# One core, fox and dilated attention step: the root table loaded first, the norm a tile ahead of V, first down weights in two halves, y stored from SP, and the dilated groups combined over two token halves

## The reference, cut to what matters

```python
xn = rmsnorm(xp, g_mix); fq, fk, fv, flf, dq, dk, dv, gf, gd = mixer_inputs(xn, pos, w_in, b_fgate)
o_fox = fox_prompt(fq, fk, fv, flf)                  # 8 heads, causal, with forget gates
for g, (win, dil) in enumerate(DIL_PATTERNS):        # (128,1), (512,4), (2048,16), 4 heads each
    o, lse = dil_group_prompt(dq[g], dk[g], dv[g], win, dil)
w = softmax(stack(lses), axis=0); o_dil = sum(w[..., None] * stack(outs), axis=0)
xp = xp + (sigmoid(gf) * (o_fox @ w_br_fox) + sigmoid(gd) * (o_dil @ w_br_dil)) @ w_mix_out
xp = xp + cross_attn(rmsnorm(xp, g_xattn), mkv, w_xq, w_xo)
u = rmsnorm(xp, g_ffn) @ w_up; gate, val = split(conv3(u) + b_conv)    # 2 x 2816 columns
xp = xp + (gelu(gate) * val) @ w_down
y = rmsnorm(xp, g_final)
```

## Time and profile before

| | |
|---|---|
| time, median of 3 runs | 2958.41 us (2953.82 to 2959.67) |
| profiled execution: its time, its span | 2956.13 us, 2954.2 us |
| mean granted TensorE clock | 0.988 |
| busy share of the span: PE, DVE, ACT, POOL | 98%, 29%, 19%, 5% |
| PE's part of the chain that ended last | 94% |
| mean DMA rate | 94 GB/s |

### The profile page before, as it was taken

One profiled execution on the slowest core, in us unless ns is written; L12 is line 12 of the kernel. 1 busy time (PEld: TensorE's weight loads), 2 busy tenths in 40 slices (PEclk: granted clock), 3 DMA queues, 4 the chain that ended last, 5 costly groups with the idle time before them and its releaser, 6 DMA issues.

```text
span 2954.2 us, 36649 instructions
## 1 busy us (share of the span) xinstructions
PE 2887.2 (98%) x14164; PEld 1836.5 (62%) x14164; DVE 843.3 (29%) x2149; ACT 562.8 (19%) x1247; POOL 146.8 (5%) x275
## 2 busy tenths in 40 slices
PE   7999999999989999999999999999999999999998
...
DMA packets 196065, 276.98 MB, mean 94 GB/s; under 512 B 20317, under 2 KB 136174, under 8 KB 194854
## 3 DMA queue, kind: packets, MB, share of 16 engines
...
...
## 4 chain that ended last, share of the span: by engine, by line
PE 94%; DMA 3%; DVE 2%; issue 1%; SPq 0%; ACT 0%; ACTq 0%; POOL 0%; DVEq 0%; POOLq 0%
PE psum L2289 22%; PE psum L2435 11%; PE psum L923 10%; PE psum L1817 8%; PE psum L1901 7%; PE psum L508 4%; PE psum L2053 4%; PE psum L678 3%; PE psum L1241 3%; PE psum L694 3%; PE psum L1825 3%; PE psum L1277 2%; PE psum L1257 2%; PE psum L705 2%; PE psum L2027 2%; DMA arena<-in_cache_fox_kv 1%
## 5 line engine op out<-in xcount | busy, mean ns | idle before, releaser
L2289 PE MATMUL psum<-arena 128*128 128x288 f32 (+1 forms) x2112 | 646.8, 470 | 0.0
L2289 PEld LDWEIGHTS psum<-arena 128*128 128x128 f32 x2112 | 402.4, 191 | 244.0 <-issue 170.2
L2435 PE MATMUL psum<-arena 128*128 128x256 f32 (+1 forms) x1760 | 327.2, 360 | 1.5 <-DMA arena<-in_w_down 1.5
L923 PE MATMUL psum<-arena 128*128 128x512 f32 (+3 forms) x960 | 316.9, 481 | 1.4 <-ACT arena L561 1.4
L2435 PEld LDWEIGHTS psum<-arena 128*128 128x128 f32 (+1 forms) x1760 | 287.9, 180 | 40.5 <-issue 3.8
L1817 PE MATMUL psum<-arena 128*128 128x368 f32 (+1 forms) x768 | 304.2, 496 | 1.7 <-ACT arena L1853 1.1
L1901 PE MATMUL psum<-arena 128*128 128x512 f32 x512 | 237.0, 596 | 0.8 <-issue 0.8
L923 PEld LDWEIGHTS psum<-arena 128*128 128x128 f32 (+1 forms) x960 | 195.0, 250 | 62.4 <-issue 35.1
L1817 PEld LDWEIGHTS psum<-arena 128*128 128x128 f32 x768 | 125.1, 193 | 68.7 <-issue 46.8
L754 DVE CUSTOM_DVE_ANT_0 arena<-psum,arena 128x256 f32<-128x256 f32 (+2 forms) x224 | 95.1, 456 | 213.7 <-PE psum L678 213.6
L728 ACT ACTIVATE arena<-arena 128x256 f32<-128x256 f32 (+4 forms) x192 | 107.5, 562 | 234.8 <-DVE arena L754 232.3
...
## 6 DMA issues: line engine op xcount, KB each, us to landing
arena<-in_cache_fox_kv SPq DMA_DIRECT2D x128, 256.0 KB, 4.4
arena<-in_cache_fox_kv ACTq DMA_DIRECT2D x128, 256.0 KB, 4.4
...
```

Source lines behind the costliest of these rows:

```text
L923: last = pe.matmul(banks[c0 // 512][p0:p0 + r, 0:n], xn_tile(k, g, t), wD[g][:, k, w0:w0 + n], start=(k == 0), stop=(k == KD - 1))
L2289: last = pe.matmul(banks[(u % 2) * 4 + x][:, 0:cw], wu[u % 3][:, k, :], xnT[:, k, c0:c0 + cw], start=(k == 0), stop=(k == KD - 1))
L2435: last = pe.matmul(banks[u % 2][p0:p0 + r, 0:n], hT(f)[:, t * P:t * P + r], wd[q % 2][:, f, c0:c0 + n], start=(f == 0), stop=(f == NF - 1))
```

## The change

Seven edits. (1) ACT does one Sqrt on a constant after its loads are issued, before the first Square. (2) norm1 becomes (-4, 68), which makes PE's order N0, N1, V0, N2, V1, N3, V2 and so on; wV comes in two halves with a semaphore each. (3) The transposes and copies of the past forget gates move from the pair j = 2 to j = 3. (4) The combination works on two halves of 512 tokens, on partitions 0 to 3 and 32 to 35: 36-column transposes for two of the groups (8 each, 16 for the third), PSUM banks of their own for the first two groups, all of the chain on 36 x 512, the head rows doubled at partition 32, and cleared statistics. (5) The last MLP unit goes over k outside the chunks and tells after k = 2 and k = 5; wd[0] is loaded in two halves at these two points, into the parts of xnT that are done with. (6) `down_pe` starts at once, waits for each half and, at the last f of the first tile, for the last gating; the four convout steps follow the tiles 1, 3, 5 and 7. (7) SP stores y in place of POOL.

```diff
         sel[hh, hh // 2, 64 * (hh % 2):64 * (hh % 2) + 64] = 1
+        sel[32 + hh] = sel[hh]
     c["head_rows"] = sel.reshape(P, -1)
...
 PLAN = dict(
-    norm1=(0, 63), v=(10, 82), p0=(82, 112), sums=(92, 93),
+    norm1=(-4, 68), v=(10, 82), p0=(82, 112), sums=(92, 93),
     p1=(112, 174), a0=(114, 176), p2=(174, 236), a1=(178, 238), p3=(236, 298), a2=(240, 300),
...
         s_clear = sem("block_diagonals_cleared")
+        stats_all = take(96 * NG, f0 + 6144 + 192)
         vrows = take(4 * P, f0).rearrange("p (a c) -> p a c", a=4)
...
                           .rearrange("p o h -> p (o h)")).then_inc(s_bfg, 16)
+            act.wait_ge(s_clear, 4)
+            act.activation(std[:, TT * 5 - 1:TT * 5], eps_t, ACT.Sqrt)
 
...
             pool.memset(eps_t, EPS).then_inc(s_clear, 1)
+            pool.memset(stats_all, 0.0).then_inc(s_clear, 1)
             pool.memset(qbF, 0.0).then_inc(s_clear, 1)
...
                 if t == 2:
-                    sp.dma_start(wV, w_in[:, :, O_FV:O_FV + 520]).then_inc(fp["wv_in"], 16)
+                    for h in range(2):
+                        sp.dma_start(wV[:, 4 * h:4 * h + 4, :],
+                                     w_in[:, 4 * h:4 * h + 4, O_FV:O_FV + 520]).then_inc(fp[f"wv_in{h}"], 16)
                 if t >= 5:
...
                 pe.wait_ge(*nth(n1, "kept", 2 * (t + 1)))
-                if t == 0:
-                    pe.wait_ge(fp["wv_in"], 16)
                 if t == 1:
...
                 for k in range(KD):
+                    if t == 0 and k % 4 == 0:
+                        pe.wait_ge(fp[f"wv_in{k // 4}"], 16)
                     xk = xnT[:, k, t * P:t * P + r]
...
                 last.then_inc(fp["computed"], 1)
-                if kind == "k" and j == 2 and n < 2:
+                if kind == "k" and j == 3 and n < 2:
                     yield now(start + 0.95 / 6.6)
...
                         pe.wait_ge(s_lf, 16 * NB * NPG)
-                        pe.wait_ge(fp["k_kept"], 6)
+                        pe.wait_ge(fp["k_kept"], 9)
                     else:
...
                         pe.wait_ge(fp["k_kept"], g)
-                    if g == 6:
+                    if g == 9:
                         pe.wait_ge(fp["lf_kept"], 2)
...
                 conv_rows_dve(dve)
-            for n in range(2 if j == 2 else 0):
+            for n in range(2 if j == 3 else 0):
                 yield now((n + 1.1) / 6.6)
...
         accT = take(NG * 2 * S, f0 + 22016).rearrange("p (g j t) -> p g j t", g=NG, j=2)
-        NM_d = [take(32, st0 + 192 + 64 * g) for g in range(NG)]
-        L_d = [take(32, st0 + 224 + 64 * g) for g in range(NG)]
+        NM_d, L_d = [[take(48, st0 + 192 + 48 * (2 * g + a)) for g in range(NG)] for a in range(2)]
+
+        def stat_place(g):
+
+            def place(i):
+                u = i // HD
+                half, x = ((u // 4, u % 4), (u % 2, u // 2), (0, u))[g]
+                return 32 * half + HD * x + i % HD
+            return place
+
 
...
             att_dil.append(attention([dil_unit(g, x) for x in range(2 * NQ)], [p[:, 0:256] for p in Pb], PT,
-                                     NM_d[g], L_d[g], GM_f, False, out_pairs, due))
-
-        stT = take(NG * 2 * S, f0).rearrange("p (g a t) -> p g a t", g=NG, a=2)
-        low = take(S, f0 + 7680)
-        den = take(S, f0 + 8704)
+                                     NM_d[g], L_d[g], GM_f, False, out_pairs, due, stat_place(g)))
+
+        HALF, RH = S // 2, 32 + HD
+        stT = take(NG * 2 * HALF, f0).rearrange("p (g a t) -> p g a t", g=NG, a=2)
+        low = take(HALF, f0 + 7680)
+        den = take(HALF, f0 + 8704)
         prod = [take(512, f0 + 9728 + 512 * i) for i in range(3)]
         cb = sems("combine", "turned natural shifted expd weighted own scaled spread product first second")
-        STAT = [psum[:, 3 * 512:5 * 512], psum[:, 5 * 512:7 * 512]]
+        STAT = [[banks[3], banks[4]], [banks[5], banks[6]], [psum[:, 3 * 512:5 * 512], psum[:, 5 * 512:7 * 512]]]
 
...
                     pe.wait_ge(fb["rows_dve"], 1)
-                if g:
-                    pe.wait_ge(cb["natural"], 2 * g)
+                    pe.wait_ge(s_clear, 4)
+                if g == 2:
+                    pe.wait_ge(cb["natural"], 4)
                 for a, st in enumerate((NM_d[g], L_d[g])):
-                    for u in range(NQ):
-                        last = pe.transpose(STAT[a][0:HD, u * P:(u + 1) * P], st[:, u * HD:(u + 1) * HD], ident)
+                    rows, n = ((RH, NQ // 2), (RH, NQ // 2), (HD, NQ))[g]
+                    for x in range(n):
+                        last = pe.transpose(STAT[g][a][0:rows, x * P:(x + 1) * P], st[:, x * HD:x * HD + rows], ident)
                 last.then_inc(cb["turned"], 1)
...
                         pe.wait_ge(cb["product"], m - 3)
-                    pe.matmul(banks[3 + m % 4], cst["head_rows"][0:HD, j * P:(j + 1) * P],
-                              stT[0:HD, g, 0, c * 512:(c + 1) * 512], start=True, stop=True).then_inc(cb["spread"], 1)
+                    pe.matmul(banks[3 + m % 4], cst["head_rows"][32 * c:32 * c + HD, j * P:(j + 1) * P],
+                              stT[32 * c:32 * c + HD, g, 0, :], start=True, stop=True).then_inc(cb["spread"], 1)
 
...
             act.wait_ge(cb["shifted"], NG)
-            act.activation(stT[0:HD, :, 0, :], stT[0:HD, :, 0, :], ACT.Exp).then_inc(cb["expd"], 1)
+            act.activation(stT[0:RH, :, 0, :], stT[0:RH, :, 0, :], ACT.Exp).then_inc(cb["expd"], 1)
 
...
                     att_over(dve, att_dil[NG - 1])
+                    dve.memset(stT[0:RH, 2, 0, :], 0.0)
+                    dve.memset(stT[0:RH, 2, 1, :], 1.0)
                 dve.wait_ge(cb["turned"], g + 1)
                 for a in range(2):
-                    dst = stT[0:HD, g, a, :]
-                    src = STAT[a][0:HD, :]
-                    if g:
-                        dst = dst.rearrange("p (i s) -> p s i", s=(1, 4, 8)[g])
-                        src = src.rearrange("p (s i) -> p s i", s=(1, 4, 8)[g])
-                    dve.tensor_copy(dst, src).then_inc(cb["natural"], 1)
-            nm = [stT[0:HD, g, 0, :] for g in range(NG)]
-            ls = [stT[0:HD, g, 1, :] for g in range(NG)]
-            lo, dn = low[0:HD, :], den[0:HD, :]
+                    if g == 0:
+                        last = dve.tensor_copy(stT[0:RH, 0, a, :], STAT[0][a][0:RH, :])
+                    elif g == 1:
+                        last = dve.tensor_copy(stT[0:RH, 1, a, :].rearrange("p (i s) -> p s i", s=4),
+                                               STAT[1][a][0:RH, :].rearrange("p (s i) -> p s i", s=4))
+                    else:
+                        halves = STAT[2][a].rearrange("p (s h i) -> p h s i", s=8, h=2)
+                        for h in range(2):
+                            last = dve.tensor_copy(stT[32 * h:32 * h + HD, 2, a, :].rearrange("p (i s) -> p s i", s=8),
+                                                   halves[0:HD, h])
+                    last.then_inc(cb["natural"], 1)
+            nm = [stT[0:RH, g, 0, :] for g in range(NG)]
+            ls = [stT[0:RH, g, 1, :] for g in range(NG)]
+            lo, dn = low[0:RH, :], den[0:RH, :]
             yield now(0.42)
...
                     pe.wait_ge(mp["uncopied"], u - 1)
-                for x, (c0, cw) in enumerate(CHUNKS):
+                if u < NU2 - 1:
+                    for x, (c0, cw) in enumerate(CHUNKS):
+                        for k in range(KD):
+                            last = pe.matmul(banks[(u % 2) * 4 + x][:, 0:cw], wu[u % 3][:, k, :], xnT[:, k, c0:c0 + cw],
+                                             start=(k == 0), stop=(k == KD - 1))
+                else:
                     for k in range(KD):
-                        last = pe.matmul(banks[(u % 2) * 4 + x][:, 0:cw], wu[u % 3][:, k, :], xnT[:, k, c0:c0 + cw],
-                                         start=(k == 0), stop=(k == KD - 1))
+                        for x, (c0, cw) in enumerate(CHUNKS):
+                            last = pe.matmul(banks[(u % 2) * 4 + x][:, 0:cw], wu[u % 3][:, k, :], xnT[:, k, c0:c0 + cw],
+                                             start=(k == 0), stop=(k == KD - 1))
+                        if k in (2, 5):
+                            last.then_inc(mp["chunk_read"], 1)
                 last.then_inc(mp["computed"], 1)
...
         def down_sp(sp):
-            sp.wait_ge(mp["computed"], NU2)
-            sp.dma_start(wd[0], w_dn[:, :, 0:256]).then_inc(dn["s"]["w_in0"], 16)
+            for h in range(2):
+                sp.wait_ge(mp["chunk_read"], h + 1)
+                sp.dma_start(wd[0][:, 11 * h:11 * h + 11, :], w_dn[:, 11 * h:11 * h + 11, 0:256]).then_inc(s_first[h], 16)
             sp.wait_ge(mp["tap2"], 2 * NU2)
...
                 sp.dma_start(wd[q % 2], w_dn[:, :, 256 * q:256 * q + 256]).then_inc(dn["s"][f"w_in{q % 2}"], 16)
+            for t in range(TT):
+                sp.wait_ge(s_out, t + 1)
```

(26 more changed lines are left out.)

20 lines of the change are left out of this document (11 added, 9 removed).

## The result

The changed kernel takes 2934.06 us (median of 5 runs, 2931.55 to 2940.43) against 2953.82 (5 runs, 2950.84 to 2959.67): ratio 0.9934, 95% interval 0.9914 to 0.9954, so a gain of 19.5 us, with 13.6 to 25.4 by the interval. These five runs of the kernel before are on the low side: in the later batches its median is 2958.2 to 2959.75. The prediction was 2933, range 2922 to 2943. The sum of its terms was 23.5 us; the two profiled executions differ by 24.6 (2956.13 and 2931.55).

The account below looks back on a forecast made before the run. PE was taken as the bound, with 94% of the chain that ended last; 4.0 + 1.8 + 5.5 + 2.4 + 9.5 + 0.3 = 23.5 us off the profiled 2956.13 gave 2932.6, predicted as 2933, range 2922 to 2943.

Parts of the forecast that it names:

- The start: Up to V2's first product: 4.0 us gained, bounds 2.0 to 4.6, with DVE's first reciprocal at 9.5.
- Past forget gates: Transposes moved a pair later: cost 0, bounds -1 to +1; left in place they would give back 4 us.
- The combination's transposes and idle time: Before the first spread: 1.8 us from 16 fewer transposes and 5.5 from the closed idle, margin 1.1.
- Rival C: Combination stays on the path, its chain on 36 x 512 no shorter than on 4 x 1024: 2940 us, chance 0.04.
- The combination's clock: After the spreads' batches: 2.4 us gained, bounds -2.0 to 9.7, with a fall of 2.4 lost after the first batch.
- Rival A: The clock holds through the combination, giving 9.7 us in place of 2.4: 2925 us, chance 0.14.
- Down: From the last MLP unit to the first down tiles: 9.5 us gained, 9.8 less 0.3 for g_final; bounds 7.0 to 9.8.
- g_final: Load that DVE's add waits for before down tile u = 2: landing near 2624, cost 0.3 us, bounds 0 and 1.5.
- the half microsecond: Sign at the down step: no wait of over half a microsecond before tile u = 2.
- The store: Last store of y, issued by a hardware queue in place of POOL: 0.3 us gained, bounds -1 to +1.
- a change of the mean clock outside the combination of over 0.002: Sign named in advance, for the whole program outside the combination: such a change would make the prediction wrong.
- Rival D: Slower: the clock falls elsewhere as edits shift 4-row and 8-row products in time; a doubled loss gives 2968 us, chance 0.03.

Follow-up runs that it names:

- s4_lf2: The changed kernel with the past forget gates turned in pair 2 again instead of pair 3: 2935.74 us (6 runs), ratio to before 0.9916.
- t2_before_rows4: The kernel before with the combination's 4-row spreads run over 128 rows, its idle of 5.48 us unchanged: 2959.18 us, one execution.
- t3_rows8: The changed kernel with only the 8-row bias products of the pair stages run over 128 rows: 2913.87 us in one execution; timed later, 2919.89 us (6 runs).
- r1_rows: The changed kernel with both the 8-row bias products and the 4-row spreads run over 128 rows, the others zero: 2918.24 us (6 runs), ratio to before 0.9864.
- r3_gfinal_first: The changed kernel with g_final's load issued ahead of the second quarter of the down weights: 2932.31 us, one execution.
- s3_down: The kernel before with only the down edits (last MLP unit over k, first weights in halves, early down tiles): 2951.25 us (12 runs), ratio 0.9972.

## Why the prediction was right, point by point

**What bounds the kernel.** PE's 94% of the chain stayed 94%, and what was edited off PE's path showed up in the time at the very end only, in the store.

**The start: 4.0, measured 3.15.** The mechanism was right, the bias row that holds the reciprocal included. Mis-sized: its landing. I took the 6.4 us of the earlier trace rows from the old issue; it was issued 0.1 later, took 7.0, and the reciprocal was at 10.13 and not 9.5. That is 0.6 of the 0.85. It should have been priced as one of many transfers in flight: over the thirteen executions in which it stayed last in ACT's queue it took 6.4 to 7.3 us. Whether the second transfer of wV slows it isn't shown; the four without edit 2 had 6.4 to 6.8.

**Past forget gates: 0, measured 0**, but with a wrong account of what happens without the edit (s4_lf2), and without the wait of up to 3.9 us that the kernel before has here in other executions.

**The combination's transposes and idle time: 7.3, measured 7.3.** The chain was priced step by step, and its end was right: with the 12.2 us won by then, the reciprocal forecast for 830.7 would be at 818.5, it is at 818.58; the first spread, forecast for 837.3, would be at 825.1, it is at 825.12. The margin was 1.3 us, forecast 1.1. Exp took 1.48 us, priced at no more than 2.76, and it didn't matter: DVE waited 3.23 us for the gate's products, ahead of the operation before the reciprocal, which is the wait that the forecast had named. Rival C (the chain no shorter) is refuted: 0.68 for an operation on 36 x 512, 3.34 for the reciprocal.

**The combination's clock: 2.4, measured 0.** This is the step that failed. It had one mean fall after the first batch and left the others as they were; in truth all four batches had one (10.26 lost against 10.25). The lower bound, -2.0, had this case. Over the eight executions with 4 and 8 rows the loss between 820 and 890 us ranges from 5.1 to 12.0; over the five of them that have edit 4, and so the same work here, it has the same range. So one execution's falls can't be carried over to the next as a sum to the tenth; a range was the right answer.

The rule of the Trainium skill (TensorE: Matmul & The Clock Gate, What's actually happening), that the gate goes by how busy PE has recently been, would, read as busy time, have had all falls go with the idle. The runs decide against that reading: those with PE busy went with the rows (t2_before_rows4, t3_rows8, r1_rows). It does hold for the fall behind the idle of 5.48 us, which stays in t2_before_rows4. Rival A (2925) is thereby refuted.

**Down: 9.5, measured 8.9.** The weights' halves were early enough. Mis-sized: g_final, 0.8 in place of 0.3, and over the half microsecond that I had named as a sign of being wrong. I had it land 13.7 less some 2 us, as one transfer fewer was ahead of it; it landed after 12.9. What holds it is the quarter of weights right ahead of it, as r3_gfinal_first shows (4.7 us when first). In the eight executions with the new order of down and g_final second it took 11.0 to 13.4 us, and PE waited 0 to 1.4: this term too was a range.

**The store: 0.3, measured 1.2** at the end of the span. It was not tried alone, but the fourteen profiles separate it: from the end of the last product to the end of the span it is 10.43 to 10.51 us in the five where POOL stores y (s3_down with the new order of down among them) and 9.21 to 9.28 in the nine where SP does. The store is issued 0.03 us after DVE's last scaling ends (2922.64 + 1.28, issue at 2923.95) and not 0.29: that is the 0.3. The rest is behind the issue, 5.55 us to the end of the span in place of 6.50, and not in the transfer, which lands after 2.9 us from either queue. It is in what POOL does once the transfer has landed: in the traces its closing DRAIN instruction takes 2.93 us in each of the five executions and 2.20 in each of the nine. Why it is shorter isn't shown. The 0.4 us by which the Trainium skill has the two paths differ to the first byte (DMA: Bandwidth & Descriptors, Specifications) isn't seen in the landing.

**What was not forecast.** The pair stages won 9.1 us, and the pages and the rest lost 6.5. I had called a change of the mean clock outside the combination of over 0.002 a refutation. Outside it, 25 us were lost before (0.012 x 2954.2 less 10.25) and 16 after (0.009 x 2929.5 less 10.26): 0.0086 and 0.0055 of the rest, a change of 0.003 (the clocks are rounded). By that criterion the account was wrong, although 5.1 us of it are the fall at the gap before down, whose part with PE at work I had counted. Rival D named the mechanism, falls that depend on where few-row products lie, and gave it one sign and 3%; it should have been a width of some 10 us to both sides around every forecast here. The profiled execution of after was a lucky one (0.991, 2.5 us under its median), and so the agreement to 1 us says less than it seems. The medians don't hang on that: 19.5 us won over all runs (13.6 to 25.4), beside 20.6 that the terms edited were measured at (3.15 + 7.3 + 0 + 8.9 + 1.2).
